# Moving the shared working area and the area at the end of on-chip memory to multiples of 128 bytes

## What is computed

```
mod = silu(c) @ w_ada + b_ada
h = modulate(rms_norm(x, norm1_w), sh1, sc1)
p = h @ w_in                       # q, k, v, z, decay, beta, short convolution, gates
o = gated_delta_rule_chunked(q, k, v, g, beta)        # 8 heads of 128
mix = (gate_a * (norm(o)*silu(z)) @ w_gdn_proj + gate_b * y_sc @ w_sc_out) @ w_o
x = x + g1 * mix;   x = x + g2 * swiglu(modulate(rms_norm(x, norm2_w), sh2, sc2))
x = modulate(rms_norm(x, normf_w), shf, scf)
# second block, layer 0: averaging over 4 windows, then a convolutional feed-forward
# layer 1: differential attention (8 heads, rotary positions), then a convolutional feed-forward
out = rms_norm(x, final_norm)
```

## Time and profile before

| | |
|---|---|
| three executions | 2199.91, 2203.62 and 2681.77 us, median 2203.62 us |
| profiled execution | span 2201.7 us, from its first to its last instruction (no other time stands beside it) |
| TensorE busy | 97% of the span, mean granted clock 0.989 |
| VectorE, ScalarE, GpSimd busy | 60%, 39%, 20% |
| DMA | 33.1% of the 16 engines' span on the main queue |

### The profile page before, as it was taken

One profiled execution on the slowest core, in us unless ns is written; L12 is line 12 of the kernel. 1 busy time (PEld: TensorE's weight loads), 2 busy tenths in 40 slices (PEclk: granted clock), 3 DMA queues, 4 the chain that ended last, 5 costly groups with the idle time before them and its releaser, 6 DMA issues.

```text
span 2201.7 us, 30260 instructions
## 1 busy us (share of the span) xinstructions
PE 2145.7 (97%) x10504; PEld 1772.8 (81%) x10504; DVE 1320.6 (60%) x1881; ACT 858.9 (39%) x1352; POOL 439.8 (20%) x336
## 2 busy tenths in 40 slices
PE   6999999999999989999999999999999999999998
PEld 3788888888888878888888888888777777888886
DVE  6777777777644454333557655633788867555431
ACT  3333333333232232322235544422566635545321
POOL 0556765557600210000110000011000000000021
PEclk8999999999999999999999999999999999999999
DMA  7344333344333323333331333333112122333332
GB/s 286 101 110 124 106 104 105 105 123 114 96 86 115 115 77 96 95 97 93 96 117 58 105 95 95 91 98 98 58 58 58 53 82 86 95 95 95 91 95 72
DMA packets 394815, 216.94 MB, mean 99 GB/s; under 512 B 7880, under 2 KB 391298, under 8 KB 393219
## 3 DMA queue, kind: packets, MB, share of 16 engines
q1 hardware_dynamic: 393939, 213.64, 33.1%
q0 software_dynamic: 288, 2.10, 0.3%
q10 hardware_dynamic: 528, 0.40, 0.1%
HBM read 211.92 MB, written 4.19 MB: 98 GB/s over the span
## 4 chain that ended last, share of the span: by engine, by line
PE 86%; DVE 8%; ACT 2%; issue 1%; DMA 1%; SPq 1%; POOL 0%; POOLq 0%; ACTq 0%; DVEq 0%
PE ps L2142 25%; PE ps L2144 25%; PE ps L2143 25%; PE ps L2315 5%; PE ps L2169 3%; DVE small L2024 1%; DVE a_sb L2057 1%; DMA ada<-w_ada 1%; DVE w_lo L1270 1%; DVE a_t_lo L2033 1%; ACT at_swap L1161 1%; DVE prob L2052 1%; ACT prob L1184 0%; PE ps L2614 0%; PE ps L2382 0%
## 5 line engine op out<-in xcount | busy, mean ns | idle before, releaser
L2142 PE MATMUL ps<-h_hi,w_hi 128*128 128x512 f32 x1896 | 770.0, 406 | 7.1 <-DVE h_lo L1334 5.5
L2144 PE MATMUL ps<-h_hi,w_lo 128*128 128x512 f32 x1896 | 743.1, 392 | 0.0
L2143 PE MATMUL ps<-h_lo,w_hi 128*128 128x512 f32 x1896 | 742.0, 391 | 0.0
L1270 DVE TENSOR_TENSOR w_lo<-raw,w_hi 128x1024 fp32r<-128x1024 f32 x331 | 429.6, 1298 | 359.5 <-ACT w_hi L779 359.1
L779 ACT ACTIVATE w_hi<-raw 128x1024 fp32r<-128x1024 f32 x336 | 355.5, 1059 | 632.7 <-PE ps L2144 583.2
L2142 PEld LDWEIGHTS ps<-h_hi,w_hi 128*128 128x128 f32 x1896 | 358.9, 189 | 77.8 <-issue 13.8
L2144 PEld LDWEIGHTS ps<-h_hi,w_lo 128*128 128x128 f32 x1896 | 357.9, 189 | 78.0
L2143 PEld LDWEIGHTS ps<-h_lo,w_hi 128*128 128x128 f32 x1896 | 359.3, 190 | 65.0
L2142 PE MATMUL ps<-act_hi,w_hi 128*128 128x512 f32 x528 | 208.5, 395 | 0.0
L2144 PE MATMUL ps<-act_hi,w_lo 128*128 128x512 f32 x528 | 207.0, 392 | 0.0
L2143 PE MATMUL ps<-act_lo,w_hi 128*128 128x512 f32 x528 | 205.0, 388 | 0.0
(11 more groups left out here) (374 smaller groups left out, 2721.2 us busy)
## 6 DMA issues: line engine op xcount, KB each, us to landing
raw<-ffn_w_up SPq DMA_DIRECT2D x88, 512.0 KB, 3.8
raw<-w_in SPq DMA_DIRECT2D x72, 512.0 KB, 3.9
raw<-w_ffn_in SPq DMA_DIRECT2D x44, 512.0 KB, 3.8
ada_w<-w_ada SPq DMA_DIRECT2D x32, 512.0 KB, 4.0
raw<-ffn_w_down SPq DMA_DIRECT2D x32, 512.0 KB, 3.7
raw<-diff_w_qkv SPq DMA_DIRECT2D x24, 512.0 KB, 3.8
ada<-w_ada SPq DMA_DIRECT2D x8, 1024.0 KB, 13.3
ada_w<-w_ada_f SPq DMA_DIRECT2D x16, 512.0 KB, 4.0
```

Of the source, the lines that this page charges most:

```text
L1270: nc.vector.tensor_tensor(w_lo[:, tile.slot], raw[:, tile.raw], w_hi[:, tile.slot].bitcast(F32), SUB)\
L2142: nc.tensor.matmul(dst, w_hi[:, tile.slot, k], hi, start=first, stop=False)
L2143: nc.tensor.matmul(dst, w_hi[:, tile.slot, k], lo, start=False, stop=False)
L2144: return nc.tensor.matmul(dst, w_lo[:, tile.slot, k], hi, start=False, stop=last)
```

## The change

The diff, whole:

```
@@ -306,6 +306,7 @@
         cst = sb("cst", [P, C_COL + 8])
+        masks_at = place[0]
         masks = sb("masks", [P, LEVELS, P])
@@ -318,12 +319,12 @@
-        work = place[0] = (place[0] + 63) // 64 * 64
+        work = place[0] = (place[0] + 127) // 128 * 128
         sq_sum = sb("sq_sum", [P, T])
         sq_tmp = sb("sq_tmp", [P, T])
         tmp = sb("tmp", [P, 6, T])
         wide = place[0]
-        end = nc.sbuf_usable_end // 64 * 64
+        end = nc.sbuf_usable_end // 128 * 128
@@ -369,8 +370,8 @@
-        pos_i = sb("pos_i", [P, T], I32, at=wide + 4096 * KF + 4096)
-        pos_f = sb("pos_f", [P, T], at=wide + 4096 * KF + 4096)
+        pos_i = sb("pos_i", [P, T], I32, at=masks_at + 1024)
+        pos_f = sb("pos_f", [P, T], at=masks_at + 1024)
```

## The result

The changed kernel takes 2210.67 us (median of 6 executions, 2208.16 to 2211.68) against 2204.07 us before (median of 6). The ratio is 1.0032, with a 95% interval of 1.0022 to 1.0042; the one execution of before at 2681.77 us is left out of it. The forecast was 2198.8 us, so the sign was wrong and the time lies just outside the range of 2191 to 2209. The profiled execution has a span of 2207.8 us, 6.1 more than before, and TensorE's busy time grew by 6.9 us while the other engines' stayed.

The account below looks back on a forecast made before the run. The prediction took TensorE's matmul pace as the bound: span 2201.7 us less 4.8 for wide matmuls gives 2196.9, plus 1.9 from span to the median of runs gives 2198.8 us, range 2191 to 2209.

Parts of the forecast that it names:

- What bounds the kernel: Whole kernel: TensorE, busy 2145.7 of 2201.7 us, so the pace at which it starts matmuls decides the time.
- The comparison of wide matmuls: DOWN, GATE, attention's projection: rest 0 by 128 gives 226.7 ns instead of 228.9, saving 4.8 us on TensorE.
- The size: Wide matmuls of DOWN, GATE and attention's projection: 720 triples at 6.7 ns, 4.8 us off TensorE.
- The rival that ended slower: DOWN and GATE: operands and weights 128 bytes apart collide, 5.4 us more, 2209.0 us; chance 8%.
- The rival with no effect: Wide matmuls: the pace belongs to the place in the program, not the address; nothing moves, 2203.6 us; chance 20%.
- the one on 256 bytes alone: Wide matmuls: a step of 256 bytes counts, so only og_ gains, 0.4 us, giving 2203.2 us; chance 10%.
- The rule: Wide matmuls: the skill's gap, 215.8 ns for 512 columns, has no address term; by it the change brings nothing.
- The narrow matmuls: Heads' 128-column matmuls: taken as 0; a rival had them gain up to 3.6 us, with chance 14%.
- VectorE, ScalarE, the positions: Other engines: counted as nothing, at most 3 ns per VectorE instruction; the positions' price is a few ns.
- DMA: Prologue, where DMA is on the path for 20.08 us: taken as 0, ends 0 and 0.5 us.

Follow-up runs that it names:

- e5_moving_only: Kernel before with act_, sc_, ao_ put 192 bytes further, work unmoved, and the changed kernel's positions and end: 2197.56 us against 2203.01, ratio 0.9976.
- e11_work_and_positions: The change without its line on end, so work and positions moved against the kernel before: 2210.44 us against 2203.31, ratio 1.0038.
- e2_all_rest0: All arrays, weights too, at multiples of 256 bytes, against the kernel before: 2197.57 us, ratio 0.9975.
- e3_weights_only: As the version with everything at multiples of 256, but raw, x and h_ keep rest 128 and the weight ring has 0: 2222.54 us, ratio 1.0090 to before.
- e1_rest128: Changed kernel with work and end set to the weights' rest, 128 by 256: 2200.83 us, ratio 0.9987 to the kernel before.
- e4_rest64: Changed kernel with work and end at rest 64 by 256, moving operands 192 bytes from the weights: 2211.95 us, ratio 1.0039 to the kernel before.
- e6_end_and_positions: The change without its line on work, so only end and positions moved against the kernel before: 2202.11 us, ratio 0.9999.
- e9_dist160: Changed kernel with work and end at rest 32 by 256, moving operands 160 bytes past the weights: 2211.61 us, one execution.

## Why the prediction was wrong, step by step

**What bounds the kernel** was right: a change of TensorE's pace in DOWN came through to the time in both directions (e5_moving_only -5.5 us, e11_work_and_positions +7.1). Beside it only the prologue, where a DMA is on the path, moved the span.

**The comparison of wide matmuls** read the trace rightly (226.7 against 228.9 ns, and 6.7 ns a triple) and named the wrong variable. That step failed: it took the rest by 128, which the change repairs, for what separates fast from slow. Its term was 4.8 us off TensorE by way of 226.7 ns in DOWN; measured were 233.3 ns and 7.0 us more for DOWN alone. What separates them is the distance to the weights by 256 bytes, as e2_all_rest0 and e3_weights_only show: the same `act_` at rest 0 is fast or slow according to where the weights lie, and `h_` turns slow when only the weights move. The layout table gave both descriptions; in the kernel before they can't be told apart, since every fast operand had both rests right. The change removes the one and makes the other worse, from 64 to 128.

**The size** of the term, once the distance is 0, was right within the noise: DOWN runs at the 226.7 ns of the sum in e1_rest128, e2_all_rest0 and e5_moving_only, and the medians fall by 2.5, 5.8 and 5.5 us for 4.8.

**The rival** that ended slower was this mechanism ("they differ by 128 bytes, as `act_`, `sc_` and `ao_` then do"). Its mark, a pace above 228.9 ns in DOWN, is what the trace shows. That its total, 5.4 us and 2209.0 us, came near the 6.6 us measured is partly luck: it priced a triple at 8.3 ns over today's and DOWN paid 3 x 4.4 = 13.2, while the prologue of the profiled execution gave 3.3 us back. I gave it 8%. The reason for so little was the count of equal observations, three stages with one number; but these three had one and the same distance, so they were one observation and said nothing on the step that the change would take. The rival with no effect has fallen with e1_rest128; the one on 256 bytes alone saw `og_` rightly and missed that the others could get worse.

**The rule** that a gap of matmuls is N / 2.4 plus 2.5 ns (the Trainium skill, TensorE: Matmul & The Clock Gate, Back-to-back issue gap), 215.8 ns here, holds for none of the eight paces, 226.7 to 234.2 ns. That section of the Trainium skill calls it the gap of a single matmul by itself, which the prediction left out, and puts a stream of weight loads and matmuls of 512 columns at about 131 ns. No pace here is near that either. Neither figure has a term for an address, and the runs show one of up to 7.5 ns.

**The narrow matmuls** I priced at 0 with a gain as the only other end. The rounds of the heads became 0.13 us longer, 1.0 us in all. All `gd_` arrays moved together, so their distance to each other stayed 0; what changed is their distance to `h_`, the weights, the identity in `cst` and all else that stayed. e5_moving_only gives the 0.13 us back with `gd_` where it was. The starts in the timeline, summed by kind of neighbours over the rounds 3 to 6, say where it lies. In the changed kernel the steps from one wide matmul to the next take 43.13 us of a round as before, those from a wide to a narrow one 6.23 us for 6.15, those between narrow ones 17.45 for 17.40. In e1_rest128, with the same round of 67.62 us, it is the wide ones that pay, 43.23 us. And distance 0, the best for the wide ones alone, isn't the best here: rounds took 67.62 us with `gd_` at distance 0 (e1_rest128, e2_all_rest0), 67.49 at 64, 67.53 at 192 (e4_rest64). Which pair of addresses in a round makes it so was not separated.

**VectorE, ScalarE, the positions** were right at nothing; for the positions e6_end_and_positions shows it within its interval.

**DMA** I took at 0 with an end at 0.5 us. In the four profiles with `ada` at a multiple of 256 bytes the DMA part of the chain ended at 32.24 to 32.59 us, in the nine others at 33.22 to 33.56: 0.6 us at least, with no overlap, and 0.8 us between before and changed. That end was too narrow, if only a little. The other 1.9 us of the prologue in the changed profile (4.76 to 2.84 us for 24 small matmuls behind it) are the granted clock, which the prediction did not look at there, and the clock doesn't go with the place of `ada`: e11_work_and_positions, with `ada` at the same place, had 0.50 from 36 to 38 us and took 4.46 us, and e9_dist160, with another, had 1.00 and took 2.84.

## What to carry to other kernels

Where TensorE is the bound and each matmul of 512 float32 columns brings its own weights, look at the addresses of both operands: moving operand and weights at the same rest by 256 bytes ran almost 3% faster (226.7 against 233.3 ns) than most other pairs. Rounding one area to a rounder number is worth nothing in itself; what counts is the difference to an array that the edit doesn't touch. And when a trace shows fast and slow cases, list every property in which they differ before choosing one, and count places that share all of them as a single observation.

## What the runs showed of the hardware beyond that

- The distance of 64 bytes is a special case between good and bad (228.9 ns), while 192, 64 bytes to the other side, is as bad as the rest (233.3 ns). Distance alone doesn't fix the pace to the last nanosecond: at 128, UP of e3_weights_only took 232.5 ns and DOWN of the changed kernel 233.3.
- The rhythm differs with the distance: the medians of the three steps of a triple with `act_` were 394, 388 and 392 ns at distance 64, 394, 395 and 396 at 128, and 389 each at 0. After a switch of distance it takes a while to settle, about ten matmuls from 64 to 0 (e6_end_and_positions), three from 128 to 0 (the changed kernel). Why two streams of reads meet this way was not shown; that they do meet is an inference from the pace.
- The eight DMAs of 1 MB into `ada`, with rows of 8,192 bytes, ended at least 0.6 us earlier when their destination in SBUF was a multiple of 256 bytes; rests of 32, 64, 96, 128, 160, 192 and 224 did not differ among themselves by more than 0.4 us. This rests on thirteen profiles of one execution each, and `x_tok`, which is loaded just before, moved along with `ada`.
